# Another order at the joins of a two-block model: steps of the experts in one run, a fifteenth weight slot, work moved between engines at three joins

## The reference

```python
def run(args):                                  # hierarchical_moe, one block of rows of one expert
    tok_b, e = args
    xb = v_pad[tok_b]                           # gather
    a, u = jnp.split(xb @ w_e_in[e], 2, axis=-1)
    return (jax.nn.silu(a) * u) @ w_e_out[e]
ys = lax.map(run, ...) * rows_w[:, None]        # gates
out = jnp.zeros((T + 1, D)).at[rows_tok].add(ys)
h = h + out[:T];  h = rms_norm(h, norm_final_w) # end of block 1
# block 2
h = h + 0.5 * rmsnorm(swiglu(rmsnorm(h, n[0]), ffn1_wi, ffn1_wo), n[1])
h = h + rmsnorm(hybrid_mixer(rmsnorm(h, n[2]), ...), n[3])
h = h + 0.5 * rmsnorm(swiglu(rmsnorm(h, n[4]), ffn2_wi, ffn2_wo), n[5])
```

## Time and profile before

| | us |
|---|---|
| median of 3 runs (2742.15 to 2747.38) | 2744.97 |
| the profiled execution | 2745.68 |
| its span | 2744.4 |
| PE busy in it | 2655.6 (97%) |
| DVE busy | 1295.1 (47%) |
| ACT busy | 889.4 (32%) |
| POOL busy | 150.1 (5%) |

### The profile page before, as it was taken

The page is one execution under the profiler, slowest core; times in us unless marked ns, Lnnn a source line. Parts: engine busy times, 40 slices in busy tenths (PEclk is TensorE's granted clock), DMA queues, the critical chain, the costliest instruction groups (busy, mean ns, idle before and its releaser), DMA issues.

```text
span 2744.4 us, 38846 instructions
## 1 busy us (share of the span) xinstructions
PE 2655.6 (97%) x16392; PEld 2076.6 (76%) x16392; DVE 1295.1 (47%) x2274; ACT 889.4 (32%) x1319; POOL 150.1 (5%) x201
## 2 busy tenths in 40 slices
PE   8999999999999999999999999999999999999997
PEld 6778888778733333349999999988879776888885
DVE  4445666544423333355344465544544434644444
ACT  4334445333221111133222243444444322431322
POOL 0000000000100000000000000031230400000000
PEclk9999999999999999999999999999999999999998
DMA  3012111134599999963222222211111122222221
GB/s 143 16 63 66 60 59 60 58 139 138 206 414 421 420 420 420 420 273 116 90 88 93 81 80 78 95 58 51 59 59 45 64 93 90 95 93 94 98 87 60
DMA packets 78204, 381.64 MB, mean 139 GB/s; under 512 B 9944, under 2 KB 10200, under 8 KB 52816
## 3 DMA queue, kind: packets, MB, share of 16 engines
q1 hardware_dynamic: 71856, 357.14, 35.1%
q0 software_dynamic: 5456, 20.11, 1.9%
q10 hardware_dynamic: 720, 1.90, 0.2%
HBM read 372.67 MB, written 10.62 MB: 140 GB/s over the span
## 4 chain that ended last, share of the span: by engine, by line
PE 79%; DMA 5%; DVE 4%; ACT 2%; issue 1%; SPq 1%; DVEq 0%; ACTq 0%
PE ps L208 77%; DMA rmore<-in_w_ein 2%; PE ps L212 1%; DMA eahead<-in_w_ein 1%; DMA ring<-in_w_ein 1%; ACT L218 1%; SPq L293 1%; DVE ringr L562 0%; PE ps L1932 0%; ACT ringr L556 0%; DMA ring<-in_w_hg 0%; DVE uT L453 0%; DVE hT L2594 0%; ACT hdd L1205 0%; DVE hT L3875 0%
## 5 line engine op out<-in xcount | busy, mean ns | idle before, releaser
L208 PE MATMUL ps<-uh,ringr 128*128 128x264 f32 (+1 forms) x2256 | 551.8, 339 | 5.8 <-DVE ringr L562 2.6
L208 PEld LDWEIGHTS ps<-uh,ringr 128*128 128x128 f32 x2256 | 364.9, 188 | 49.9 <-issue 5.0
L208 PE MATMUL ps<-buh,ringr 128*128 128x512 f32 (+1 forms) x1312 | 346.6, 350 | 9.2 <-ACT hg L1187 8.1
L208 PE MATMUL ps<-uTr,ringr 128*128 128x512 f32 (+1 forms) x1136 | 349.9, 345 | 0.0
L562 DVE TENSOR_TENSOR ringr<-ring,ringr 128x1024 fp32r<-128x1024 f32 (+1 forms) x217 | 260.5, 1210 | 146.3 <-ACT ringr L556 145.8
L556 ACT CAST ringr<-ring 128x1024 fp32r<-128x1024 f32 (+1 forms) x217 | 221.6, 1036 | 103.7 <-DMA ring<-in_w_fi 45.5
L208 PEld LDWEIGHTS ps<-buh,ringr 128*128 128x128 f32 x1312 | 218.3, 188 | 40.3 <-issue 12.2
L208 PEld LDWEIGHTS ps<-uTr,ringr 128*128 128x128 f32 x1136 | 197.1, 189 | 22.5 <-issue 3.1
L2040 DVE TENSOR_TENSOR hT<-hT,ps 128x512 f32<-128x512 f32 x128 | 87.8, 688 | 182.0 <-PE ps L208 180.9
L208 PE MATMUL ps<-ful,ringr 128*128 128x264 f32 (+1 forms) x648 | 169.4, 322 | 0.0
L208 PE MATMUL ps<-fhh,ringr 128*128 128x264 f32 (+1 forms) x612 | 132.1, 321 | 0.0
(11 more groups left out here) (478 smaller groups left out, 4568.6 us busy)
## 6 DMA issues: line engine op xcount, KB each, us to landing
eahead<-in_w_ein SPq DMA_DIRECT2D x48, 1024.0 KB, 22.7
rmore<-in_w_ein SPq DMA_DIRECT2D x44, 1024.0 KB, 23.2
ring<-in_w_ein SPq DMA_DIRECT2D x36, 1024.0 KB, 24.1
ring<-in_w_fi SPq DMA_DIRECT2D x54, 512.0 KB, 3.7
rmore<-in_w_eout SPq DMA_DIRECT2D x26, 1024.0 KB, 26.4
eahead<-in_w_eout SPq DMA_DIRECT2D x22, 1024.0 KB, 26.2
fmore<-in_w_fi SPq DMA_DIRECT2D x34, 512.0 KB, 3.7
ring<-in_w_hg SPq DMA_DIRECT2D x32, 512.0 KB, 3.8
```

What stands on the lines that cost most here:

```text
L208: return self.P.matmul(out, lhsT, rhs, start=start, stop=stop, skip_group_check=True)
```

## The change

1. *Slots.* `xg` has two gather buffers instead of three and the pad behind it is gone; `Experts` gets 11 slots of `rmore` in place of 10. The first is lent on its own, free once the transposes out of `oh` are done.
2. *Experts.* The four steps of an expert stand in one run between `turn_pe` and the out product, on banks 1, 3, 5, 7; the in product has bank 2, the out product bank 6. The last pair's output is split expert by expert. The casts 1 and 2 and all three rests of the first FFN weights move behind the experts' output.
3. *Join.* 8 filler products instead of 18; four steps, then one behind each of t = 0 to 3; `first3` waits for casts and rests weight by weight; gathers of squares stand between the low parts.
4. *FFN slots.* `fmore` is lent in front of the ring, and `ahead_act(0, 5)` casts two more weights before the root.
5. *Second FFN.* Weights 4, 5, 6 go to banks 1, 3, 5, and the 32 filler products are gone.
6. *Decays.* The logits stand behind the second group's first product in bank 6, `act1`/`dve1` at j = 1, `pe2`/`act2`/`dve2` at j = 2 in bank 7; the 22 filler products are gone.

```diff
+def first3(k, W, parts, banks, ws, xh, xl, r0, r1):
+    cols = list(enumerate(split(r0, r1)))
+    k.P.wait_ge(*parts.high.at(1))
+    for i, b in enumerate(banks):
+        k.P.wait_ge(*W.cast.at(i + 1))
+        for j, (c0, c1) in cols:
+            k.mm(k.ps[:, b + j, 0:c1 - c0], ws[i][0][0], xh[0][:, c0:c1], True, False)
+    k.P.wait_ge(*parts.low.at(1))
...
+    for i, b in enumerate(banks):
+        k.P.wait_ge(*W.rest.at(i + 1))
...
-        self.raw, self.xg = mix.oh, sb("xg", [128, 3, D])
-        sb("rpad2", [128, D])
+        self.raw, self.xg = mix.oh, sb("xg", [128, 2, D])
...
-        k.lend(*(x[:, 0:more - EARLY, :] for x in k.both("rmore", [128, more, SLOT], st)), *free)
+        both = k.both("rmore", [128, more, SLOT], st)
+        k.lend(*(x[:, 0:1, :] for x in both), route.rturn.at(4))
+        k.lend(*(x[:, 1:more - EARLY, :] for x in both), *free)
...
-        return {"x": (0, 0), "in": (2, 3), "h": (4, 4), "out": (6, 7), "to": (1, 5)}[what][e % 2]
+        if what == "to":
+            return (1, 3, 5, 7)[e % 4]
+        if what == "in" and e == 1:
+            return 3
+        return {"x": 0, "in": 2, "h": 4, "out": 6}[what]
...
                 self.turn_pe(e - 1)
-                for n in self.steps(e)[3:]:
+                for n in self.steps(e):
                     self.to_pe(n)
...
             ins.then_inc(used.next(), 1)
-            if beside and c:
-                self.to_pe(beside[c - 1])
...
             if e == NE:
-                for i in range(3):
-                    self.ahead.cast_act(i)
+                self.ahead.cast_act(0)
...
+                if e > NE - 2:
+                    A.wait_ge(*self.y_act.at(e))
+                    A.copy(self.yh[q % 2][p:p + 64, 0:512], self.yb[q % 2][p:p + 64, 0:512]).then_inc(self.high.next(), 1)
...
+        self.ahead.cast_act(1)
+        self.ahead.cast_act(2)
...
             if e == NE:
-                for i in range(3):
-                    self.ahead.rest_dve(i)
-            if e:
+                self.first_rest_dve()
+                self.second_rest_dve()
+            elif e:
...
+    def second_rest_dve(self):
+        k, V = self.k, self.k.V
+        y, yh, yl = (x[1][64:128] for x in (self.yb, self.yh, self.yl))
+        out = k.ps[64:128, self.bank("out", NE - 1), :]
+        V.wait_ge(*self.outof.at(2 * NE))
+        V.tensor_copy(yh[:, 512:1024], out).then_inc(self.split.next(), 1)
+        V.wait_ge(*self.split.last())
+        V.tensor_tensor(yl[:, 512:1024], out, yh[:, 512:1024].bitcast(F32), SUB).then_inc(self.y_dve.next(), 1)
+        V.wait_ge(*self.high.at(NE // 2 + 1))
+        V.tensor_tensor(yl[:, 0:512], y[:, 0:512], yh[:, 0:512].bitcast(F32), SUB).then_inc(self.low.next(), 1)
...
         add = lambda m: exp.add_dve(4 * NE - 8 + m)
+        add(0)
         V.wait_ge(*self.mhigh.at(1))
         V.tensor_tensor(self.lo[:, :, 0:NM], um, k.uh[:, :, 0:NM].bitcast(F32), SUB).then_inc(self.mlow.next(), 1)
-        add(0)
         add(1)
-        for m in range(6):
-            add(m + 2)
+        self.low_dve(0)
+        for i in range(3):
+            W.rest_dve(i)
+        add(2)
+        for m in range(1, 8):
+            if m < 6:
+                add(m + 2)
             self.low_dve(m)
...
+            if m >= 3:
+                self.gather_dve(m - 3)
+            if m == 5:
+                W.rest_dve(3)
+        for m in range(5, 8):
+            self.gather_dve(m)
...
-        self.k.busy(0, 18)
-        for m in range(6):
+        self.k.busy(0, 8)
+        for m in range(4):
             exp.to_pe(4 * NE - 8 + m)
...
-        if t in (1, 2):
-            self.exp.to_pe(4 * NE - 3 + t)
+        if 0 < t < 5:
+            self.exp.to_pe(4 * NE - 5 + t)
...
-            exp = Experts(k, st2, route, 10, free, end, W)
+            exp = Experts(k, st2, route, 11, free, end, W)
...
-        k.lend(*k.both("fmore" + name, [128, 3, SLOT], st), *free, last=True)
+        k.lend(*k.both("fmore" + name, [128, 3, SLOT], st), *free)
...
             norm.sum_pe()
-            k.busy(1, 32)
             return
...
-                    self.bank[i] = b = k.pair(4)
+                    if r0 and i < 7:
+                        b = 2 * i - 7
+                        k.take(b)
+                    else:
+                        b = k.pair(4)
+                    self.bank[i] = b
...
         k, r0, W, nxt = self.k, self.r0, self.W, self.nxt
+        W.ahead_act(0, 5)
         self.norm.root_act()
...
-        self.bank["logit"] = b = k.pair()
-        k.busy(b + 1, 22)
+    def logits_pe(self):
+        k, P = self.k, self.k.P
+        self.bank["logit"] = b = 6
+        k.take(6)
         P.wait_ge(*self.row_out.at(1))
...
+                if j == 1 and x == 0:
+                    dec.logits_pe()
...
-            if j == 1:
+            if j == 2:
                 dec.pe2()
```

More of the change, by code:

```diff
@@ L578, in halves_pe, with columns @@
         self.k.P.wait_ge(*self.rest.at(i + 1))
+        return self.columns(i)
+    def columns(self, i):
         n = self.size[i] // 128
@@ L1849, in __init__ @@
         sig = k.sig
-        self.got = [sig.pdma(f"got{i}") for i in range(3)]
+        self.got = [sig.pdma(f"got{i}") for i in range(2)]
         self.xturn, self.hturn, self.into, self.outof = sig.pe("xturn"), sig.pe("hturn"), sig.pe("into"), sig.pe("outof")
@@ L1899, in pe @@
                 self.product_pe("in", e, self.xT[:, e % 2], self.chunk_in(e), 4, self.x_out.at(e + 1), self.into,
-                                self.steps(e), self.prod.at(e + 1))
+                                self.prod.at(e + 1))
                 if e == 0:
                     self.nxt.meta_pe()
-            else:
-                for n in self.steps(e)[0:3]:
-                    self.to_pe(n)
             if e + 1 < NE:
@@ L1918, in to_pe @@
         if m == 0:
-            k.P.wait_ge(*self.low.at(q + 1))
+            k.P.wait_ge(*self.low.at(q + 2 if q == NE // 2 - 1 else q + 1))
             k.P.wait_ge(*self.ones.at(q + 1))
@@ L1929, in rows_pe, with product_pe @@
         q, p = e // 2, slice(64 * (e % 2), 64 * (e % 2) + 64)
-        k.P.wait_ge(*self.got[q % 3].at(16 * (q // 3 + 1)))
+        k.P.wait_ge(*self.got[q % 2].at(16 * (q // 2 + 1)))
         for x in range(8):
-            ins = k.P.transpose(k.ps[:, b, 64 * x:64 * x + 64], self.xg[p, q % 3, 128 * x:128 * x + 128], k.ident[p, p])
+            ins = k.P.transpose(k.ps[:, b, 64 * x:64 * x + 64], self.xg[p, q % 2, 128 * x:128 * x + 128], k.ident[p, p])
         ins.then_inc(self.xturn.next(), 1)
         k.give((b,), self.x_out.at(e + 1))
-    def product_pe(self, what, e, x, chunk, n, ready, used, beside, *free):
+    def product_pe(self, what, e, x, chunk, n, ready, used, *free):
         k, b = self.k, self.bank(what, e)
@@ L2017, in dve @@
                                        op0=MUL, op1=MUL).then_inc(self.prod.next(), 1)
-            for n in self.steps(e)[3:]:
+            if e == NE - 1:
+                V.tensor_scalar(self.to[:, 1, :], self.route.row, pair[:, NE // 2 - 1:NE // 2], None, ALU.is_equal).then_inc(
+                    self.ones.next(), 1)
+            for n in self.steps(e):
                 self.add_dve(n)
             if e == NE:
-                for i in range(3):
-                    self.ahead.rest_dve(i)
-            if e:
+                self.first_rest_dve()
+                self.second_rest_dve()
+            elif e:
                 q, p = (e - 1) // 2, 64 * ((e - 1) % 2)
@@ L2044, in first_pool @@
         self.k.G.wait_ge(*self.route.indexed.at(1))
-        for q in range(3):
+        for q in range(2):
             self.gather_pool(q)
@@ L2049, in pool @@
         k, G = self.k, self.k.G
-        for q in range(3, NE // 2):
-            G.wait_ge(*self.xturn.at(2 * (q - 3) + 2))
+        for q in range(2, NE // 2):
+            G.wait_ge(*self.xturn.at(2 * (q - 2) + 2))
             self.gather_pool(q)
@@ L2241, in act @@
             if m == 3:
+                k.table(ACT.Ln)
                 W.cast_act(3)
@@ L2257, in dve, with gather_dve @@
         add = lambda m: exp.add_dve(4 * NE - 8 + m)
+        add(0)
         V.wait_ge(*self.mhigh.at(1))
         V.tensor_tensor(self.lo[:, :, 0:NM], um, k.uh[:, :, 0:NM].bitcast(F32), SUB).then_inc(self.mlow.next(), 1)
-        add(0)
         add(1)
-        for m in range(6):
-            add(m + 2)
-            self.low_dve(m)
[L2265 to L2276, removed]
+        self.low_dve(0)
[5 more added lines that the diff above has]
+                add(m + 2)
+            self.low_dve(m)
+            if m >= 3:
[4 more added lines that the diff above has]
+            self.gather_dve(m)
+    def gather_dve(self, m):
+        k, V = self.k, self.k.V
+        sq, w = self.squares[:, m, :], k.fin[:, 0, m:m + 1]
+        V.wait_ge(*self.square.at(m + 1))
+        if m:
+            V.wait_ge(*self.gathered.at(m))
+            V.scalar_tensor_tensor(out=self.acc, in0=sq, scalar=w, in1=self.acc, op0=MUL, op1=ADD).then_inc(
```

(12 more changed lines are left out.)

39 lines of the change are left out of this document (27 added, 12 removed).

## The result

The changed kernel takes 2753.36 us (median of 7 runs, 2748.54 to 2757.53) against 2747.38 (7 runs, 2742.15 to 2749.06) for the kernel before: ratio 1.0025, interval 1.0015 to 1.0035. It is slower by 6.0 us; 13.8 us faster was forecast. In the 32 runs taken beside the first four experiments the kernel before stands at 2747.4, so the three runs known at the prediction, 2744.97, were 2.4 on the low side. The profiled execution spans 2752.0 us, against 2744.4.

A forecast was written before the change was run, and what follows sets the result against it. Experts were taken as bound by weight transfers at 420 GB/s with PE close behind, PE setting the end elsewhere. Terms 3.2 + 0.6 + 2.1 + 6.9 + 1.0 = 13.8 us off 2744.97 gave 2731.2, likeliest range 2728 to 2734.5.

The forecast's parts named there:

- Parts 1 and 2: Experts: fifteenth slot fills the transfers' pause, steps in one run, outputs split singly; -3.2 us, bounds -4 and -0.7.
- Part 3: Join to the first FFN: first step 2.1 us sooner, PE then waiting for rests; -0.6 us, bounds -2.1 and +1.5.
- Part 4: First FFN: weights 4 to 6 land early, cast and split in idle time, no pause; -2.1 us, bounds -2.1 and -1.
- Part 5: Second FFN: weights 4 and 5 start at once, weight 6 sooner; -6.9 us, bounds -8.0 and -2.5.
- Part 6: Convolutions: decays later, -1.9 us without the clock, +0.9 for half a clock fall; -1.0, bounds -3.4 and +1.
- The prediction's own sign: Second FFN: forecast is wrong if weights 4 and 5 start later than 0.5 us behind the sum.
- The rival "weights not ready": FFNs: `fmore` not filled, cast and split ahead of the root; gains shrink to 1 and 2.5 us, 2736.7 us; chance 10%.
- the rival of a low clock at every join: Where fillers went, PE starts at 1.2 GHz, 1.7 us in full each at three places; 2735.4 us, chance 11%.

The follow-up runs named there:

- the first four experiments: Changed kernel with casts made, with bank order restored, or with ones put back; kernel before with experts and join alone: 2739.55, 2747.63, 2748.57, 2745.56 us.
- the ten: Profiled executions of kernels with fifteen slots; from a start ahead of the diff to the end of out(31) they took 643.7 to 645.8 us, mean 644.8.
- experiment 9: Repaired kernel without lending the fifteenth slot, so 14 slots as before: 2737.31 us, ratio 0.9967.
- experiment 1: Changed kernel with weights 4 and 5 of both FFNs really cast ahead of the root: 2739.55 us, ratio 0.9972.
- experiment 3: Changed kernel with the 32 products of ones put back behind the sum of the second FFN: 2748.57 us, ratio 1.0006.
- experiments 2 and 4: 2: changed kernel, `k.turn` moved on by 2 at the second mixer's output products, 2747.63 us; 4: kernel before with experts' part and join alone, 2745.56 us.
- experiment 7 with 20 ones: Repaired kernel plus 20 products of ones in the pause ahead of weight 5 of the convolutions: 2737.75 us, ratio 0.9966.
- the repaired kernel: Changed kernel with weights 4 and 5 really cast ahead and `k.turn` moved on by 2 at the second mixer's output products: 2734.50, then 2738.61 us.

## Why the prediction was wrong

*Parts 1 and 2 (-3.2).* Right in kind, 0.8 too much: -2.4 in the mean of the ten, by experiment 9 nearly all of it the slot. PE was to be under the transfers, and it is: its last in-chunk waits for DMA. The gain of DVE's order at the end, 0.8, is there (out(31) ends 12.08 us behind the last in-chunk, 12.86 before). But experiment 9 has it too, and its stage is only 0.1 shorter than before: from PE's start to the last in-chunk it took 0.7 longer. The run of steps and the two gather buffers, put at no cost, may be the reason; with one execution against a scatter of 2.1 between those with fifteen slots, no run shows it.

*Part 3 (-0.6).* -1.05; the first step at 2.4 as worked out, the rests cost two waits of 0.6 instead of three.

*Part 4 (-2.1), the first step that failed.* "land, are cast and split in the idle stretches of ACT and DVE": they landed, but were not cast, and the term was zero. I took the name and arguments of `ahead_act(0, 5)` for what it does, and did not work out its condition with the order as it is when that line runs. With the casts made it is -2.0 (experiment 1).

*Part 5 (-6.9), the step that turned the sign.* "Now weights 4 and 5 (cast ahead) go into banks 1 and 3 at once": the same false premise. It cost the gain, and beyond it 4.1, of which 2.7 is the clock (experiment 3). The prediction's own sign came up: weight 4 starts 7.76 us behind the sum, where over 0.5 was to mean wrong. The rival "weights not ready" named this way of failing and priced it at -2.5, as if the ones were still there: with them gone it is +4.1. With the casts made the stage gave -5.5: the -6.9 less 0.4 for `first3`, and 1.0 more. At weight 6 all of it is still there: PE starts it 12.96 us behind the start of the sum, 20.01 before. The 1.0 goes at the first out product of the last group, by a wait that the kernel before doesn't have and all ten executions with weights 4 to 6 in named banks do (PE, experiment 1):

```profile
2687.15 0.47 PE L208 MATMUL ps<-fhh,fmore2r 128*128 128x512 f32 x1 [0.83 <-issue]
```

The profile names no releaser, but the code gives one. Weights 4, 5 and 6 no longer turn the counter, so it stands at 57 there instead of 60. The out product takes banks 0 and 1 either way (`k.pair(3)`), but the last product in front of it now has bank 0 (56 in turns of 4) instead of bank 6 (59), and DVE reads that product (L2622) from 2686.36 to 2687.05. No run tried it with the counter put right.

*Part 6 (-1.0).* -1.9 without the clock, as worked out. The clock is no half term but one or the other: behind the pause of 2.69 us it fell in four profiled executions of eight (6.8 us once, 3.4 us three times) and stayed up in four. Nor does the length of the pause order it, as the prediction took it to: at the pause of 2.0 us in front of weight 4 of the first FFN, which left the clock up in the kernel before, it fell in two of six (experiments 2 and 4, 3.4 us).

*What the sum lacked.* The two `k.pair()` that part 6 removes also turn the counter for everything behind it, until it is set to 0 for the second FFN: +2.6 in a stage that the diff does not touch. Part 5 does the same to the counter within the second FFN, the 1.0 above. No step spoke of either, though the diff shows the calls go.

*The clock.* I gave the rival of a low clock at every join 11% and priced it at 1.7 per place; 1.5 per fall of 3.4 us is what was measured, but the pause of 7.76 brought 10.2 us of it. At the join with 8 ones instead of 18 it came once in eleven executions (experiment 7 with 20 ones, 28.18 us instead of 26.65). The rule that I cited, that TensorE is throttled by default and activity releases it (the Trainium skill, "TensorE: Matmul & The Clock Gate", section "What's actually happening"), speaks against taking filler away; the traces agree at the pauses of 5.09 and 7.76 us, where the clock was low in every execution that had them (three and two).

The stages of the repaired kernel sum to -2.4 - 1.0 - 2.0 - 5.5, and -0.4 to -1.9, that is -11.3 to -12.8 on 2747.4; measured, by the two ratios, are -12.9 and -9.3. It beats both kernels.

## What to carry to other kernels

A helper with a condition in it is to be worked out at the place where it is called, with the state it then finds: an early-work call may emit nothing, and the filler that covered for it is gone all the same. Price a failed premise with everything else in the change as it will be, fillers removed included. And whoever takes a user out of a rotating counter moves every later user; look for the places behind, not only for those in the diff. Here that happened twice.

## What the runs showed of the hardware

One program, the kernel with both repairs, showed a fall of the clock behind the pause of 2.69 us in one profiled execution and none in the other. Over all kernels with that pause it fell in four executions of eight, behind the pause of 2.0 us in two of six, and around the pause of 1.00 us in front of the second mixer's output stage (at 2261.84 in the kernel before) in eight of thirteen. The falls there lasted 3.4 us, or once 6.8; 10.2 us were seen at the pause of 7.76. One of 3.4 us with PE busy behind it costs 1.5. Whether fewer fillers also widen the spread of times is not shown: the 32 runs of the kernel before span 12.2 us by themselves.
